# Where the nest of conditional expert tiles ends: four or six register-addressed tiles behind it

## What is computed

```
logits = xf @ w_router + b_router            # 32 experts
top_v, top_i = top_k(logits, 4); gates = softmax(top_v)
for every chosen (token, expert):
    hmid = x @ w_up[e] + b_up[e]             # w_up[e]: 1024 x 2048
    hg = min(hmid[:, :1024], 7); hl = clip(hmid[:, 1024:], -7, 7)
    act = hg * sigmoid(1.702 * hg) * (hl + 1)
    y += gate * (act @ w_down[e] + b_down[e])  # w_down[e]: 1024 x 1024
```

## Time and profile before

| | |
|---|---|
| median of three runs | 1553.96 us (1553.16 to 1554.0) |
| profiled execution | 1554.18 us, its span 1552.4 us |
| TensorE busy | 1369.8 us, 88% of the span |
| VectorE, ScalarE, GpSimd busy | 637.1, 211.5, 269.0 us |
| weights of the experts, up and down | 256 + 256 transfers by SyncE |
| mean rate of DMA | 300 GB/s over the span |
| mean granted TensorE clock | 0.94 of full speed |

### The profile page before, as it was taken

How to read it: one execution, slowest core, us unless ns; L and a number is a source line. 1 busy time by engine, 2 the same in 40 slices (tenths; PEclk the granted TensorE clock), 3 DMA queues, 4 the chain that set the end, 5 groups by cost and what they waited for, 6 DMA issues and landing times.

```text
span 1552.4 us, 31165 instructions
## 1 busy us (share of the span) xinstructions
PE 1369.8 (88%) x12283; PEld 720.0 (46%) x12284; DVE 637.1 (41%) x1422; ACT 211.5 (14%) x560; POOL 269.0 (17%) x321
## 2 busy tenths in 40 slices
PE   7999999999898989769999997797797997977876
PEld 5778777778787434223333332332242332322322
DVE  2999755553572252214242422221232332221222
ACT  2111242414240111000000000000000000000001
POOL 2008700224220010102121211110111111110100
PEclk9999999999999999889999998998898999998997
DMA  8888678304027689999969999999999999999796
GB/s 189 123 174 133 103 117 129 114 9 110 1 103 251 254 356 416 417 414 399 404 282 368 401 415 411 416 416 412 413 409 407 410 400 414 411 412 414 307 410 267
DMA packets 136204, 466.19 MB, mean 300 GB/s; under 512 B 12334, under 2 KB 67254, under 8 KB 103271
## 3 DMA queue, kind: packets, MB, share of 16 engines
q1 hardware_dynamic: 135839, 463.37, 83.4%
q0 software_dynamic: 48, 0.85, 0.2%
q10 hardware_dynamic: 192, 0.13, 0.0%
HBM read 457.84 MB, written 7.34 MB: 300 GB/s over the span
## 4 chain that ended last, share of the span: by engine, by line
PE 63%; DMA 17%; DVE 5%; issue 5%; SPq 4%; POOL 3%; DVEq 1%; ACT 0%; POOLq 0%
PE psum L1242 18%; DMA arena<-in_w_up 16%; PE psum L1254 9%; PE psum L737 9%; PE psum L1210 5%; PE psum L1228 3%; PE psum L1276 3%; DVE acc L1814 3%; PE psum L1129 2%; PE psum L1219 2%; SPq L440 2%; PE psum L1137 2%; PE psum L820 2%; SPq L437 2%; POOL acc L535 2%
## 5 line engine op out<-in xcount | busy, mean ns | idle before, releaser
L1242 PE MATMUL psum<-arena,gate 128*32 128x512 f32 x3264 | 408.4, 631 | 124.5 <-DMA arena<-in_w_up 124.5
L2341 DVE COPY gate<-psum 128x256 f32<-128x256 f32 x51 | 21.7, 425 | 655.3 <-PE psum L1254 655.3
L1242 PEld LDWEIGHTS psum<-arena,gate 128*32 128x32 f32 x3264 | 97.9, 112 | 392.9 <-issue 285.4
L737 PE MATMUL psum<-arena 128*128 128x304 f32 (+1 forms) x1024 | 262.6, 419 | 3.4 <-DMA arena<-in_w_in 1.9
L737 PEld LDWEIGHTS psum<-arena 128*128 128x128 f32 x1024 | 196.5, 192 | 67.2 <-issue 2.4
L1254 PE MATMUL psum<-arena,gate 128*32 128x256 f32 x3264 | 189.5, 384 | 2.8 <-DMA arena<-in_w_down 1.8
L659 POOL TENSOR_TENSOR qkv<-qkv 128x192 f32<-128x192 f32 x50 | 80.8, 1616 | 632.6 <-DVE qkv L2303 632.6
L1254 PEld LDWEIGHTS psum<-arena,gate 128*32 128x32 f32 x3264 | 100.9, 110 | 87.2 <-issue 22.0
L1814 DVE SCALAR_TENSOR_TENSOR acc<-arena,pcol,acc x240 | 126.3, 608 | 0.0
L1210 PE MATMUL psum<-qkv 128*32 128x256 f32 (+1 forms) x1224 | 86.2, 396 | 0.7 <-DVE qkv L2266 0.7
L1697 ACT ACTIVATE gate<-psum 128x256 f32<-128x256 f32 x51 | 19.5, 383 | 477.9 <-PE psum L1219 477.9
(11 more groups left out here) (419 smaller groups left out, 1287.8 us busy)
## 6 DMA issues: line engine op xcount, KB each, us to landing
arena<-in_w_up SPq DMA_DIRECT2D x256, 1024.0 KB, 12.1
arena<-in_w_down SPq DMA_DIRECT2D x256, 512.0 KB, 8.6
arena<-in_w_in SPq DMA_DIRECT2D x32, 1024.0 KB, 10.5
arena<-in_w_conf_out SPq DMA_DIRECT2D x4, 1024.0 KB, 5.1
arena<-in_state_dn_S SPq DMA_DIRECT2D x8, 512.0 KB, 7.3
arena<-in_w_dn_out SPq DMA_DIRECT2D x1, 4096.0 KB, 14.3
out_ss<-arena SPq DMA_DIRECT2D x8, 512.0 KB, 6.2
arena<-in_w_out SPq DMA_DIRECT2D x1, 4096.0 KB, 17.1
```

Source lines behind the costliest of these rows:

```text
L737: last = mm(bank[2 * (j % 2) + f][:, 0:cols.stop - cols.start], wring[:, slot, k, P * half:P * (half + 1)], rhs[:, k, cols], start=(k == 0 ...
L1242: last = mm(hidden(q)[v], xgT[:, i, SL * q0:SL * (q0 + 1)], parts(wup[k], q)[v], start=False, stop=(k == KC - 1), skip_group_check=True)
```

## The change

One constant changes, `LAST`, and with it `FIXED` goes from 28 to 26. The conditional nest keeps its 35 tiles and starts at tile 26 in place of 28; with 19 extra tiles it ends behind tile 44 in place of 46, and tiles 45 to 50 are register-addressed, where 47 to 50 were. The same is so on all four computing engines. SyncE's stream doesn't change.

```diff
@@ -41,7 +41,7 @@
 XB = ((T - META) * TOPK - NE) // SL
 NT = NE + XB
 NMORE = -(-(T - META) // SL) - 1
-LAST = 4
+LAST = 6
 FIXED = NE - LAST
 N_INFO = 1 + NT + NE
 HALF = 512
```

## The result

The median of five runs is 1546.38 us (1542.91 to 1548.58) against 1553.96 us (1553.16 to 1555.45), a ratio of 0.9947 with a 95% interval of 0.9935 to 0.9958: 7.6 us faster, inside the range of 1543.6 to 1548.2, 1.3 us above the point of 1545.1. The profiled execution took 1544.52 us with a span of 1542.6, so that execution was 9.7 us faster than the profiled one before; it is 1.9 us under the changed kernel's own median, so the profile flatters the change. Single executions of the changed kernel differ by up to 5.7 us.

What follows compares the result with a forecast made beforehand. Bound: single-buffered weight loads and TensorE gate each other, with a 9.58 us hole at tile 47. From 1553.96 us, -9.4 regained and +0.5 toll, jump 0, sum to -8.9, so 1545.1 us; range 1543.6 to 1548.2.

Steps and rivals of the forecast that it cites:

- The hole of 9.58 us: TensorE at tile 47: a taken branch over 16 unused tiles costs 6.35 us, the low clock after it 3.23.
- DMA's side of it: Expert 29's down weights requested late, at 1461.59; DMA idles 9.1 us from 1452 to 1464; gain taken -9.4 us.
- The twin of tiles 25 to 27: Same expert pattern as tiles 45 to 47 without the stall; shifted by 399.9 us, it puts the down issue at 1452.04.
- The jump, "cost taken: 0": Jump moved before tile 45, where TensorE waits 8.66 us for weights; a stall up to about 10 us is hidden.
- the same price there: Jump before tile 45 delays its bias matmul by 6.35 us, as at tile 47, to 1404.17.
- the bound above: Lower clock lasting longer after the jump, slowing tile 44's down matmuls; up to 1.9 us lost.
- A wait of 1 to 2 us for weights behind it: Sign expected at tile 45: up-weight wait behind the jump of 1 to 2 us in place of 8.66.
- The toll, +0.5 us: TensorE reads the extra-tile count and passes the first comparison before tile 26, now uncovered; between 0 and 0.61 us.
- A stall that waits for the queue: Rival: instruction fetch before tile 45 waits behind queued weights; full wait 1565.5 us, chance 0.03; scaled 1552.5, 0.02.
- A stall that doesn't move: Rival: the stall belongs to tile 47's place, not the jump; only the toll remains, 1554.5 us; chance 0.04.
- A DMA that regains only half: Rival: DMA regains half of its 9.1 us idle time after 1452; 1549.9 us; chance 0.04.
- The longer jump, twice the price: Rival: jump before tile 45 takes 12.1 us, passing the 10 us of cover by 2.1; 1547.2 us; chance 0.04.

Runs made afterwards that it cites:

- the run with ten reads: Changed kernel with ten more register reads on TensorE right behind the jump, before tile 45; 1550.25 us, ratio 0.9976 against the kernel before.
- the run with nine reads: Changed kernel with eight more reads of the number of extra tiles on TensorE before tile 26; 1552.21 us, ratio 0.9985 against the kernel before.

## Why the prediction was right, point by point

- **The hole of 9.58 us.** Right in cause, place and size. Tile 46 to 48 fell by 9.58 us in the first profile of the changed kernel and by 9.57 in the second, and by 9.9 if the second profile of the kernel before is the measure; taking the branch away with all else as before gave 9.8 us in the median.
- **DMA's side of it.** The twin of tiles 25 to 27 told the issue time: 1452.04 was derived, 1452.5 named with the toll, 1451.81 measured. That the absolute times meet so closely is luck, as the second profile of the changed kernel has its issue at 1456.56; counted from tile 46 it came 9.56 us earlier, 9.55 were derived. The 12 us window moved 393 GB/s where at least 350 were named for each 4 us.
- **The jump, "cost taken: 0".** The place was covered, as I had it; the price was wrong. The step that put "the same price there" took 6.35 us from another landing place. It measured 11.48 us, since the target moved with the code to the end of a fetched piece. It stayed hidden because the cover is deeper than I had it: 1.7 us beyond the 11.5 by the run with ten reads, where I had a branch of 10 us, which is a bias matmul 10.3 us late. The sum had missed that TensorE is quicker once it needn't wait between chunks. The first half took 1.94 + 1.79 + 1.07 + 1.93 = 6.73 us of work and takes 5.56 behind the stall, and tile 44's down matmuls start 1.9 us after it, where they started 2.5 us after it. So the bound above, a lower clock that lasts longer, went the other way. That the stall stayed hidden was luck as much as argument: the earlier trace rows can't tell where in its piece a target lies. "A wait of 1 to 2 us for weights behind it" failed for the same reason, and came (0.84 us) once the code was shifted.
- **The toll, +0.5 us.** The size is borne out only through the run with nine reads, at 0.6 to 0.8 us lost for each us that TensorE is late there, which makes 0.4 to 0.5. That "each ns that the issue is late is lost" was a little too strong.
- **-8.9 against -7.6.** The point is 1.3 us too good. With both groups of runs of the changed kernel it is -7.6 and -6.8, without the jump at tile 45 -8.9. That may be a rest of the jump's price that reaches the end in some executions, which I had bounded at 1.9 us and taken as 0. The profiles neither show it (tile 44 to 46: 60.45 us with the jump, 60.13 without, 60.40 and 60.70 in the kernel before) nor exclude it, and the intervals overlap. It stays open.
- **The rivals.** A stall that waits for the queue fell: 6.18 us with 29 us of weights queued, the same as with 11, and 6.31 us for the whole stall once the code was shifted. A stall that doesn't move fell: the hole went from tile 47 to where the jump was put, and the branch is 65 to 73 ns where nothing is jumped over. A DMA that regains only half fell too: at 393 GB/s, 12 x (1 - 393/415) = 0.6 us are left of the 9.1 without work. The longer jump, twice the price, nearly came true, as a stall of 11.48 us, and was hidden where its working had 2.1 us of it show.

## What to carry to other kernels

Here the far taken branch cost about 6 us in nearly every place it was put, so put such a branch where its engine waits for something else anyway, and look at what stands behind that wait. Find such a place by a twin: the same pattern of work elsewhere in the trace without the stall tells both what would be regained and whether another stream can follow. A place found this way is right for one set of data; here one tile fewer behind the nest takes back 5 us of the 7.6, and two more take back 3.

## What the runs showed of the hardware

- TensorE's jump over the code of 16 tiles took 6.05 to 6.23 us in ten profiles and 7.33 in an eleventh, no longer with 29 us of weights queued than with 11. No other distance was tried. VectorE's took at most 63 ns; its tile has some 11 operations where TensorE's has over 360 matmuls and weight loads, so it jumps over far less code. That this is the reason wasn't tried.
- Where the target lies in its fetched piece matters: four or five instructions before the end it cost 5.1 us more (11.48 and 11.26 us of stall in two profiles), and 12 instructions of shift took that away (6.31).
- After 5.7 to 6.3 us without work TensorE's granted clock was 0.50 to 0.51 in the first 4 us of work, the lower of its two levels, in the three profiles in which this was read (the first of the kernel before, the one shifted by 36 instructions, the one with nine reads); the tile took 3.2, 2.9 and 1.9 us longer.
- A branch back over the body of one tile, some 380 instructions, took 0.21 us (median of 19, 0.22 at most).
- The Trainium skill, page "Runtime: NRT & Kernel Launch", section "Instruction fetch mechanics", puts the fetch in 16 KB blocks of 256 instructions. The packets of 0.02 MB and what the shift did agree with the blocks; that one holds 256 instructions no run here shows.
